# First transfers on one queue, row sums by GpSimd from the columns of x, first head norms block by block

## The reference

```
h = rms_norm(x, norm_gain)                 # x * rsqrt(mean(x*x) + eps) * gain
proj = h @ w_in                            # 1024 x 8448, in column panels
qa, ka, va, qb, kb, vb, ga, gb, mg = split(proj)
qa = head_rms_norm(qa) * scale             # per head of 64: y * rsqrt(mean(y*y) + eps) * gain
ka = head_rms_norm(ka); qb, kb likewise
... attention, gates, output projection, then the two layers
```

## Time and profile before

| | |
|---|---|
| median of three runs | 1159.21 us |
| the profiled execution's own time | 1158.94 us |
| its span, first to last instruction | 1157.1 us |
| TensorE busy | 1141.3 us, 99% |
| VectorE busy | 823.7 us, 71% |
| ScalarE busy | 586.4 us, 51% |
| GpSimd busy | 137.2 us, 12% |
| mean granted TensorE clock | 0.996 of full |

### The profile page before, as it was taken

How to read it: one execution, slowest core, us unless ns; L and a number is a source line. 1 busy time by engine, 2 the same in 40 slices (tenths; PEclk the granted TensorE clock), 3 DMA queues, 4 the chain that set the end, 5 groups by cost and what they waited for, 6 DMA issues and landing times.

```text
span 1157.1 us, 15957 instructions
## 1 busy us (share of the span) xinstructions
PE 1141.3 (99%) x6207; PEld 950.2 (82%) x6207; DVE 823.7 (71%) x1245; ACT 586.4 (51%) x736; POOL 137.2 (12%) x152
## 2 busy tenths in 40 slices
PE   7999999999999999999999999999999999999997
PEld 6888777787998777878888888998777878888886
DVE  5565656666689899787777454599899787777443
ACT  6445565644436666633555333525776534555332
POOL 1222231100003143000000000003234000000000
PEclk9999999999999999999999999999999999999999
DMA  9545543457545668654555555545677654655640
GB/s 362 193 171 206 194 186 121 175 185 275 171 153 201 208 182 223 195 183 163 184 190 197 212 188 188 177 152 216 187 213 220 182 182 146 218 183 186 217 161 37
DMA packets 35323, 219.34 MB, mean 190 GB/s; under 512 B 3888, under 2 KB 5680, under 8 KB 10928
## 3 DMA queue, kind: packets, MB, share of 16 engines
q1 hardware_dynamic: 32800, 204.67, 50.6%
q0 software_dynamic: 1728, 12.58, 5.8%
q10 hardware_dynamic: 720, 1.06, 0.3%
HBM read 217.25 MB, written 1.05 MB: 189 GB/s over the span
## 4 chain that ended last, share of the span: by engine, by line
PE 81%; issue 15%; DVE 1%; ACT 1%; DVEq 1%; DMA 1%; POOL 0%; POOLq 0%; ACTq 0%
PE panel L921 35%; PE panel L925 17%; PE panel L992 5%; PE tile L1006 4%; PE panel L995 3%; PE panel L969 3%; PE panel L968 3%; PE panel L967 3%; PE heads_out L1346 1%; PE heads_out L1200 1%; PE tile L1260 1%; PE tile L1369 1%; PE tile L1366 1%; DMA area<-in_x_columns_dram 1%; DVEq L2058 1%
## 5 line engine op out<-in xcount | busy, mean ns | idle before, releaser
L630 DVE TENSOR_TENSOR ring_parts<-ring,ring_parts 128x2048 fp32r<-128x2048 f32 (+2 forms) x172 | 389.8, 2271 | 161.5 <-ACT ring_parts L596 155.6
L596 ACT ACTIVATE ring_parts<-ring 128x2048 fp32r<-128x2048 f32 (+2 forms) x184 | 346.8, 1888 | 255.1 <-PE panel L925 203.8
L921 PE MATMUL panel<-ring_parts,hT 128*128 128x512 f32 (+2 forms) x1344 | 329.2, 392 | 4.0 <-issue 2.7
L921 PEld LDWEIGHTS panel<-ring_parts,hT 128*128 128x128 f32 x1344 | 241.2, 189 | 60.3 <-issue 12.7
L921 PE MATMUL panel<-ring_parts,area_parts 128*128 128x512 f32 x736 | 178.5, 391 | 0.0
L925 PE MATMUL panel<-ring_parts,hT 128*128 128x512 f32 (+2 forms) x672 | 170.4, 388 | 0.0
L921 PEld LDWEIGHTS panel<-ring_parts,area_parts 128*128 128x128 f32 x736 | 138.1, 188 | 29.5
L925 PEld LDWEIGHTS panel<-ring_parts,hT 128*128 128x128 f32 x672 | 121.2, 188 | 25.5 <-issue 2.5
L992 PE MATMUL panel<-hT,ring_parts 128*128 128x512 f32 x512 | 129.9, 393 | 0.0
L2205 DVE SCALAR_TENSOR_TENSOR area<-area,cw 128x256 f32<-128x256 f32 x240 | 104.7, 497 | 2.9
L992 PEld LDWEIGHTS panel<-hT,ring_parts 128*128 128x128 f32 x512 | 91.6, 189 | 16.0
(11 more groups left out here) (248 smaller groups left out, 1133.0 us busy)
## 6 DMA issues: line engine op xcount, KB each, us to landing
ring<-in_w_layers_dram SPq DMA_DIRECT2D x140, 1024.0 KB, 4.9
ring<-in_w_first_dram SPq DMA_DIRECT2D x38, 1024.0 KB, 5.0
ring_parts<-in_w_layers_dram POOLq DMA_DIRECT2D x12, 1024.0 KB, 8.7
ring<-in_w_first_dram SPq DMA_DIRECT2D x5, 512.0 KB, 10.1
area<-in_second_bias_dram SPq DMA_DIRECT2D x8, 320.0 KB, 3.2
ring<-in_w_layers_dram SPq DMA_DIRECT2D x4, 560.0 KB, 4.0
area<-in_first_bias_dram SPq DMA_DIRECT2D x4, 384.0 KB, 4.4
area<-in_later_bias_dram SPq DMA_DIRECT2D x1, 1536.0 KB, 12.2
```

Of the source, the lines that this page charges most:

```text
L596: act.activation(ring_lo[:, SLOTS + hi, 0:w], ring[:, slot, 0:w], ACT.Copy).then_inc(high_ready, 1)
L630: g.tensor_tensor(ring_lo[:, slot, 0:w], ring[:, slot, 0:w], ring_lo[:, SLOTS + hi, 0:w], ALU.subtract).then_inc(low_ready, 1)
L921: pe.matmul(ps[:, b, 0:width], t[:, 4 * i + k, b * P:(b + 1) * P], hi[:, k, :], start=(i == k == 0 and t is of[0]), stop=False)
```

## The change

Four things change, all in the first 30 us of the program.

- **First transfers.** The gains and chunk 0 of x are one array now and one transfer, issued by ACT. The other seven chunks are issued by SP, between the pieces of qa's weights: weights of chunk 0, chunk 1, weights of chunk 1, chunks 2 and 3, their weights, and so on. x in rows is no longer loaded here.
- **Row sums.** POOL squares each chunk of x in columns and adds the squares up into one 128x256 tile (eight multiplications and seven additions). TensorE multiplies that tile by a column of -1, one product for each block, just before its last two products of qa (`row_sums`). VectorE changes the sign and signals POOL, which makes the row factor as before. ScalarE's row squares go.
- **First head norm.** For qa alone, ScalarE squares the panel without the row factor, and VectorE multiplies the head sums by the square of the factor afterwards. POOL's root is made for each block by itself, in all eight panels, and VectorE normalises a block as soon as its root is there. Two calls of `lows_to` move behind the head sums and behind the normalising of qa.
- **Small things.** Nine warm-up products read 512 columns of zeros instead of 640; the scaling of two gain columns moves from VectorE's beginning to just before the sums; a PSUM tile "xs" is added to the turns.

The core of the diff:

```
-X_CHUNKS = ((0, 1), (1, 2), (2, 4), (4, 8))
+X_CHUNKS = ((0, 1), (1, 2), (2, 4), (4, 6), (6, 8))
...
         def _(sp):
             for n, (i, s, end) in enumerate(QA_CHUNKS):
+                if n:
+                    cs, ce = X_CHUNKS[n]
+                    sp.dma_start(x_columns()[:, cs:ce, :], a["x_columns"][:, cs:ce, :]).then_inc(columns_loaded[n], 16)
...
-            for b in range(NB):
-                sp.dma_start(x[:, b, :], sorted_x[b]).then_inc(x_loaded[b], 16)
...
+                row_sums()
                 low_weights(KC - 1)
+            def row_sums():
+                ps, done = tile_for(part, "xs")
+                pe.wait_ge(x_summed, 1)
+                for b in range(NB):
+                    mm = pe.matmul(ps[:, 2 * b:2 * b + 2], x[:, 0, b * P:(b + 1) * P], minus_one, start=True, stop=True)
+                mm.then_inc(done, 1)
...
-            act.dma_start(first[:, :], a["first"]).then_inc(loaded, 16)
-            for i, (s, end) in enumerate(X_CHUNKS):
-                act.dma_start(x_columns()[:, s:end, :], a["x_columns"][:, s:end, :]).then_inc(columns_loaded[i], 16)
+            s, end = AREA_1["first"][0], AREA_1["x0"][1]
+            act.dma_start(area[:, s:end], a["first"]).then_inc(columns_loaded[0], 16)
...
-            for b in range(NB):
-                act.wait_ge(x_loaded[b], 16)
-                row_squares(b, b)
...
+                        if n == 0:
+                            act.activation(squares_of[:, b, 0:w], ps[:, b, 0:w], ACT.Square).then_inc(head_sq, 1)
+                        else:
+                            act.activation(squares_of[:, b, 0:w], ps[:, b, 0:w], ACT.Square, scale=rstd[:, b:b + 1]).then_inc(head_sq, 1)
...
+            sums = tile_of(v, part, "xs")[:, 0:2 * NB].rearrange("p (b n) -> p b n", b=NB)
+            v.tensor_scalar(ss, sums[:, :, 0], -1.0, None, ALU.mult).then_inc(tile_sem(part, "xs"), 1)
+            v.drain().then_inc(squares, 2)
...
+                        if n == 0:
+                            v.drain()
+                            v.wait_ge(rstd_ready, 1)
+                            r = v.tensor_scalar(hs[:, b, 0:nh], hs[:, b, 0:nh], rstd[:, b:b + 1], rstd[:, b:b + 1], ALU.mult, ALU.mult)
+                        r.then_inc(head_sum, 1)
                     if n == 0:
-                        lows_to(part, "qa/1")
+                        lows_to(part, "qa/0")
...
-                    v.wait_ge(head_rstd, n + 1)
                     for b in range(NB):
+                        v.wait_ge(head_rstd, NB * n + b + 1)
...
+                    if n == 0:
+                        lows_to(part, "qa/1")
...
+            total, squared_chunk = x[:, 0, 0:TOKENS], x[:, 1, :].rearrange("p (s t) -> p s t", s=4)
+            for k in range(KC + 1):
+                if k < KC:
+                    wait_columns(g, k)
+                    to = squared_chunk[:, k % 4, :] if k else total
+                    g.tensor_tensor(to, x_chunk(k), x_chunk(k), ALU.mult).then_inc(x_squared, 1)
+                if k > 1:
+                    g.wait_ge(x_squared, 2 * k - 2)
+                    s = g.tensor_tensor(total, total, squared_chunk[:, (k - 1) % 4, :], ALU.add)
+                    s.then_inc(x_summed if k == KC else x_squared, 1)
...
-                inverse_root(hr[:, :, 0:nh], hs[:, :, 0:nh], 1.0 / HD, head_rstd,
-                             half_power[:, 0:nh].unsqueeze(1).broadcast_to([P, 2, nh]))
+                for b in range(NB):
+                    g.wait_ge(head_sum, NB * n + b + 1)
+                    if n >= 1:
+                        g.wait_ge(head_normed, NB * (n - 1) + b + 1)
+                    inverse_root(hr[:, b, 0:nh], hs[:, b, 0:nh], 1.0 / HD, head_rstd, half_power[:, 0:nh])
```

More of the change, by code:

```diff
@@ L216, in plan_tiles @@
     return out
-FIRST_TILES = ([t for p in NORMED for t in transposed(p)] + plan_tiles(FIRST_PLAN, units_first())
+FIRST_TILES = (["xs"] + [t for p in NORMED for t in transposed(p)] + plan_tiles(FIRST_PLAN, units_first())
                + by_columns("m") + by_columns("n"))
@@ L301 @@
     ("mgt", 4096), ("L", 4 * 1024), ("PT", 2 * 1024), ("E", 2 * 2 * TOEP)])
+AREA_1["first"] = (END_1, END_1 + FIRST)
+AREA_1["x0"] = (END_1 + FIRST, END_1 + FIRST + TOKENS)
+END_1 += FIRST + TOKENS
 AREA_2, END_2 = area_map([
@@ L365, in block_kernel @@
         par = sb("par", PAR)
-        first = sb("first", FIRST)
         cw = sb("cw", 4, TAPS)
@@ L393, in one @@
             return area[:, s:e]
+        first = one("first")
         def two(name):
@@ L444, in block_kernel @@
         rope_loaded = sem("rotation_loaded")
-        x_loaded = [sem(f"x{b}_loaded") for b in range(NB)]
+        x_squared = sem("squares_of_x_columns_step")
+        x_summed = sem("squares_of_x_columns_summed")
         x_again = sem("x_in_natural_order_loaded")
@@ L634, in x_columns, with x_chunk, wait_columns @@
             return one("mgt")[:, 0:KC * TOKENS].rearrange("p (k t) -> p k t", k=KC)
+        def x_chunk(k):
+            return x_columns()[:, k, :] if k else one("x0")
+        def wait_columns(eng, k):
+            for i, (s, _) in enumerate(X_CHUNKS):
+                if s == k:
+                    eng.wait_ge(columns_loaded[i], 16)
         def qa_parts(k):
@@ L1466, in _ @@
             part = part_1
-            act.dma_start(first[:, :], a["first"]).then_inc(loaded, 16)
-            for i, (s, end) in enumerate(X_CHUNKS):
-                act.dma_start(x_columns()[:, s:end, :], a["x_columns"][:, s:end, :]).then_inc(columns_loaded[i], 16)
+            s, end = AREA_1["first"][0], AREA_1["x0"][1]
+            act.dma_start(area[:, s:end], a["first"]).then_inc(columns_loaded[0], 16)
             act.wait_ge(pad_ready, 1)
             act.activation(stat[:, 254:255], zero, ACT.Identity)
-            act.wait_ge(loaded, 16)
             for k in range(KC):
[L1474 to L1477, removed]
+                wait_columns(act, k)
+                act.activation(hT_hi[:, k, :], x_chunk(k), ACT.Identity, scale=first[:, k:k + 1]).then_inc(columns_high, 1)
                 for n, (i, s, end) in enumerate(QA_CHUNKS):
@@ L1830, in _ @@
             v.memset(minus_one, -1.0).then_inc(pad_ready, 1)
[L1831 to L1834, removed]
             lows = [0]
@@ L1898, in _ @@
                 v.wait_ge(columns_high, k + 1)
-                v.scalar_tensor_tensor(hT_lo[:, k, :], x_columns()[:, k, :], first[:, k:k + 1], hT_hi[:, k, :], ALU.mult, ALU.subtract)\
+                v.scalar_tensor_tensor(hT_lo[:, k, :], x_chunk(k), first[:, k:k + 1], hT_hi[:, k, :], ALU.mult, ALU.subtract)\
                  .then_inc(columns_low, 1)
@@ L1910, in _ @@
             v.tensor_tensor(fold[0:4 * N_CMP, :], ident[0:4 * N_CMP, 0:2 * N_CMP], ident[0:4 * N_CMP, 2 * N_CMP:4 * N_CMP], ALU.add)
-            v.wait_ge(rstd_ready, 1)
+            for c in (8, 10):
+                e = v.tensor_scalar(first[:, c:c + 1], first[:, c:c + 1], HD ** -0.5, None, ALU.mult)
+            e.then_inc(cw_ready, 1)
+            sums = tile_of(v, part, "xs")[:, 0:2 * NB].rearrange("p (b n) -> p b n", b=NB)
+            v.tensor_scalar(ss, sums[:, :, 0], -1.0, None, ALU.mult).then_inc(tile_sem(part, "xs"), 1)
+            v.drain().then_inc(squares, 2)
             lows[0] = HI_SLOTS
@@ L2029, in _ @@
                         lows_to(part, f"{FIRST_PANELS[n - 1]}/1")
-                    elif s == 6:
+                    elif s == 6 and n:
                         lows_to(part, f"{p}/0")
@@ L2742, in pack @@
     first_bias, second_bias, later_bias = bias_tables(f["rel_bias"], f["rel_table_2"])
+    gains_first = by_partition(f["norm_gain"][0])
     x_sorted = f["x"][0].reshape(P // 2, NB, 2, D).transpose(1, 0, 2, 3).reshape(TOKENS, D)
+    x_columns = x_sorted.T.reshape(KC, P, TOKENS).transpose(1, 0, 2)
     return dict(
-        x=f["x"][0], x_columns=x_sorted.T.reshape(KC, P, TOKENS).transpose(1, 0, 2), w_first=w_first, w_layers=np.stack(w_layers), par=np.stack(par),
-        first=np.concatenate([by_partition(f["norm_gain"][0]), gains, np.tile(f["sink_a"][0:1], (P, 1))], 1),
+        x=f["x"][0], x_columns=x_columns, w_first=w_first, w_layers=np.stack(w_layers), par=np.stack(par),
+        first=np.concatenate([gains_first, gains, np.tile(f["sink_a"][0:1], (P, 1)), x_columns[:, 0]], 1),
         first_bias=first_bias, second_bias=second_bias, later_bias=later_bias, b_merge=f["b_merge"][0].reshape(-1),
```

22 lines of the change are left out of this document (8 added, 14 removed).

## The result

The changed kernel takes 1164.13 us (median of 6 runs, 1163.71 to 1164.62) where the kernel before took 1158.24 beside it (6 runs, 1157.47 to 1159.25): ratio 1.005, interval 1.004 to 1.006. It is 5.9 us slower, above the range of the forecast. The profiled execution took 1164.29 with a span of 1162.5.

What follows compares the result with a forecast made beforehand. TensorE, busy 99%, was taken to bound the kernel, so front gains pass through one for one. R moves by -0.6: profiled 1158.94 becomes 1158.3, and the median, 0.27 above, 1158.6 us; range 1155.2 to 1162.2.

Steps and rivals of the forecast that it cites:

- The first transfer: At the start: gains and first chunk of x, in one 138 KB transfer, land at 5.1 us, between 4.5 and 6.7.
- The operation on GpSimd: Row sums in the front: one 128x256 square or sum on POOL takes 0.65 us, bounds 0.21 and 1.485.
- the turns: qa's chunk loop: VectorE and POOL alternate, needing 1.85 us a chunk from the third on, where TensorE needs 1.36.
- Rival B: Front: POOL's squares run beside VectorE without turns; 3.4 us faster, or 1.86 more with the clock up: 1153.9; chance 0.10.
- D: Rival, front: a dearer POOL operation, each 0.1 us adding 1.2; at 0.95 the time is 1162.2; chance 0.16.
- Q: The moment the products of qa end: 21.06 us in the kernel before, predicted 20.4.
- The chain to R: From qa's end to qb0: factor ready 23.1, roots 25.3 and 27.25, block 1 normalised 28.05, TensorE 0.16 later.
- R: The moment TensorE starts qb0: 28.79 us in the kernel before, predicted 28.2.
- The clock, left as now: After the standstill ahead of qb0: it stays about 2.05 us long, so the slow stretch was left unchanged.
- Rival C: After the standstill ahead of qb0: turns occur but the clock stays up, 1.86 us more gained, 1156.7; chance 0.14.
- The rest at nothing: Fewer ScalarE squares, shorter clearing, block-wise roots of later panels (0.7 more each) and idle VectorE were counted as costing nothing.
- the forecast by itself: Whole kernel: turns at about 0.65 us, clock as now, giving 1157.2 to 1160.6 us; chance 0.60.

Runs made afterwards that it cites:

- e1: The changed kernel with 20 unused columns where `first` had been, putting the area back at byte 127360: 1158.11 us, ratio 0.9996 to the kernel before.
- e9: e1 plus five drains on VectorE at its start: 1157.87 us, ratio 0.9995 to the kernel before.
- e7: e1 with GpSimd's head root made for both blocks at once, as before the change: 1161.56 us, ratio 1.003 to the kernel before.
- e11: e1 with 32 unused columns ahead of the ring, moving ring, hT and area by 128 bytes with distances kept: 1158.14 us, ratio 1.0001 to the kernel before.
- e6: e1 with row sums by ScalarE from rows of x, loaded between kava's halves, and no GpSimd squares: 1157.86 us, ratio 0.9996 to the kernel before.
- e8: e1 with chunks 1 to 7 of x issued by ACT, so SP issues weights alone: 1159.58 us, ratio 1.0009 to the kernel before.
- e5: e1 with GpSimd squaring and adding only chunks 0 and 1 of x: 1156.69 us, ratio 0.9987 to the kernel before.
- e4: The kernel before with 64 unused bytes ahead of `cw`, so the area starts at byte 127424: 1162.77 us, ratio 1.0036.
- e3: The kernel before with 32 unused bytes ahead of `cw`, so the area starts at byte 127392: 1164.23 us, ratio 1.0045.
- e2: The kernel before with `first` allocated last, so the area starts at byte 127264 as in the changed kernel: 1163.65 us, ratio 1.0043.
- e10: e1 with 32 unused columns inside the area, ahead of the branches: 1156.19 us, ratio 0.9985 to the kernel before.
- e12: e6 with the 32 unused columns of e10 ahead of the branches: 1154.53 us, ratio 0.9969 to the kernel before.

## Why the prediction was wrong, by its steps

*The first transfer (5.1)*: right. ScalarE starts on chunk 0 at 5.01.

*The operation on GpSimd (0.65) and the turns (1.85 us a chunk)*: right. VectorE and GpSimd of the kernel after, 13 to 16 us, a timeline each:
```profile
14.31 0.96 DVE L1915 SCALAR_TENSOR_TENSOR hT<-area,hT 128x256 fp32r<-128x256 f32 x1
15.20 1.10 DVE L1922 TENSOR_TENSOR ring_parts<-ring,ring_parts 128x512 fp32r<-128x512 f32 x1
```
```profile
13.23 0.61 POOL L2575 TENSOR_TENSOR x<-area 128x256 f32<-128x256 f32 x1
13.81 1.18 POOL L2578 TENSOR_TENSOR x<-x 128x256 f32<-128x256 f32 x1
14.96 0.79 POOL L2575 TENSOR_TENSOR x<-area 128x256 f32<-128x256 f32 x1
```
Alone an operation takes 0.61; beside VectorE both stretch, and a chunk takes 15.27 - 13.37 = 1.90. Rival B is out, and so is D.

*Q (20.4)*: 0.6 too early. The turns were to bind from chunk 2 on; in the trace the weights of chunk 4 land at 12.68 and start the last stretch of turns. The term that was short is the landing, on a queue slower than before's: the turns end at 20.22 where 19.8 was said. The last two products and their semaphore took 0.79 where 0.60 was said.

*The chain to R*: right. The rows that answer to the earlier trace rows, first VectorE, then GpSimd:
```profile
23.23 0.29 DVE L2000 TENSOR_SCALAR stat<-stat 128x8 f32<-128x8 f32 x1 [0.77 <-POOL stat L2584]
...
24.39 1.22 DVE L634 TENSOR_TENSOR ring_parts<-ring,ring_parts 128x1024 fp32r<-128x1024 f32 x1
...
27.70 0.75 DVE L2010 SCALAR_TENSOR_TENSOR tok<-panel,stat 128x512 f32<-128x512 f32 x1 [1.18 <-POOL stat L2568]
```
```profile
22.95 0.24 POOL L2584 TENSOR_SCALAR stat<-stat 128x2 f32<-128x2 f32 x1
...
23.99 1.67 POOL L2568 TENSOR_TENSOR stat<-stat 128x8 f32<-128x8 f32 x1
...
26.03 1.64 POOL L2568 TENSOR_TENSOR stat<-stat 128x8 f32<-128x8 f32 x1
```
The factor is ready at 23.19 (said 23.1), the first root at 25.66 (25.3), the second at 27.67 (27.25), block 1 normalised at 28.45 (28.05), R at 28.61 (28.2). The Trainium skill, "SBUF — State Buffer" (Who interferes with whom), would have had VectorE's subtraction wait out the power. It ran its usual 1.22 inside the power's 1.67, so the row was the right choice for a narrow operation, while the 128x256 operations in the loop take turns as that section says.

*The clock, left as now*: wrong. It did not fall in the profiled run of this kernel, and the six runs lie within 0.9 us of each other, less than a fall costs; of 28 runs of before 16 read a mean of 0.997 or less. What decides it is open: e1 and e9 have the same front and standstills of 1.72 and 1.73, and it fell in e9's profiled run only. Rival C had this, at 0.14; its gain came as 1.6 (5.50 less 3.92 on the 16 products) where 1.86 was said.

*The rest at nothing*: this is the step that failed. That sentence cleared the edits it named, and the move of `first` into the area was not among them. The move was priced as a transfer and never as an allocation. It costs 6.0 us (after against e1): some 824 products at 6.5 ns and 288 at 0.9 make 5.6. Without it the forecast stands: e1 took 1158.11 where 1158.6 was said. But it stands by luck, through two misses that cancel: rival C's gain of 1.6, and the new waits for the logits, at which e1 loses 1.2 matmul against matmul (1.1 us of waits in after). So the front's gain did not go through to the end one for one, as the prediction took it; VectorE's pauses behind these waits were not in the sum either. A slip on which nothing rests: by its own price, 1.2 us for each 0.1, the forecast by itself is 1157.4 to 1160.4, not 1157.2 to 1160.6.

## What to carry to other kernels

An edit of a tensor's place or size moves every tensor allocated behind it; list the start addresses before and after, as one lists instructions, and compare the spacing of the matmuls with `xN` rows of the same line. Here operands that start a multiple of 256 bytes from the weights they meet gained 2 to 3% on each product of 512 columns, for a few unused columns. And where TensorE stands still ahead of a long run of products, price the clock behind the standstill as well as the standstill: in the profiled run of e7 it cost 2.74 us beside 1.83.

## What the runs showed of the hardware

- The distance between the two operands of a product in SBUF, modulo 256 bytes, sets the spacing of 128x512 products at full clock: 226.8 ns at 0, 229.0 at 192, 232.4 at 128, 233.3 at 32, 64 and 160. It showed only with both moved (e11) that it is a distance. Of the products with hT, also at distance 0, most stand at 227 too (the median); why over a quarter take 231 or more, which makes their mean 228.7, is open.
- VectorE's pauses of some 0.4 us, which nothing in the profile releases, sit at places of its program, 64 past a multiple of 128 of its records in the trace, and fall on other instructions when some are added ahead of them (e9).
- One queue with packets of 2 and 4 KB moved 258 to 352 GB/s from 7 to 13 us with no work on GpSimd, two queues 355 to 416 (e6, e8).
- After the standstill ahead of qb0 the clock fell in the profiled runs with 1.74 (e6), 1.73 (e9), 1.98 (before) and 3.31 us (e7), and stayed up with 1.08 (e5), 1.37 (e4, e8), 1.42 (e3), 1.56 (e11), 1.70 (e2), 1.72 (after, e1) and 1.73 (e10, e12). So its length alone does not decide.
